# Row buffers, work between tiles, and crossed inverse rounds in a hybrid decoder trunk

## The chip, the cores and the metric

The kernel runs on one core of a Trainium2 chip. Its time is the device time of one execution in microseconds (us); lower is better. Before the change three runs gave a median of 3220.76 us (3219.93 to 3223.76).

The engines are named as the profile names them: PE is the matrix engine (PEld its weight loads), DVE the vector engine, ACT the scalar engine, POOL the general one, SP the queue that issues most transfers. Each engine runs its own instruction stream in order; the streams meet at semaphores.

## The reference, cut to what matters

One layer of a decoder with two recurrent branches. A prompt of 16 meta tokens and 512 tokens and eight samples of four tokens (560 rows in all) are normalised by rows, multiplied by one large weight matrix, sent through an RWKV-7 branch and a gated linear attention branch, merged, and projected back.

```python
h = _rms_norm(x, norm_pre[l])            # x * rsqrt(mean(x*x) + eps) * g
z = h @ w_in[l]                          # 2048 x N_COLS
...
def step(S, inp):                        # RWKV-7, one token, per head
    r_t, w_t, k_t, v_t, a_t, b_t = inp
    sa = jnp.einsum('nhvk,nhk->nhv', S, a_t)
    S = S * w_t[:, :, None, :] + sa[..., None] * b_t[:, :, None, :] + v_t[..., None] * k_t[:, :, None, :]
    return S, jnp.einsum('nhvk,nhk->nhv', S, r_t)
```

The kernel computes the RWKV recurrence by chunks of 64 tokens. Inside a chunk the terms `sa` of all tokens hang on each other through a strictly triangular 64 x 64 matrix, so each chunk needs the inverse of (identity minus that matrix), for each of 32 heads.

## The kernel before

The program is five blocks, one after the other, each closed on all engines before the next begins. Block A normalises and transposes the rows, block B projects the two low-rank columns of the RWKV branch, block C is the attention branch, block D the RWKV branch in 16 turns of two heads each, block E the output projection.

All large products are done in three passes of a split precision: a weight tile `raw` is rounded to `w_hi` by ACT (`split_hi`, L181) and the rest is put in `w_lo` by DVE (`split_lo`, L189); the activations are split likewise into `act_hi` and `act_lo`. One call of `next` on the generator `steps` (L191 to L206) issues the three matmuls of one of 16 slices of the depth, 280 columns each (L203, L204, L205). A weight tile has 32 such steps.

**Block A** (L230 to L400) goes over five tiles of 128 rows (the last has 48). There are two row buffers `x_in`. SP loads the norm's weights first, then tiles 0 and 1, and each later tile only after the tile two before it has been transposed. `square_root(t)` on ACT squares a tile in four pieces of 512 columns; DVE adds the four sums (L346); ACT takes the root (L317); DVE takes the reciprocal and scales the row (`normalise`, L349 and L353). PE transposes (L392) into four banks, ACT rounds to `act_hi` (L326), DVE subtracts to `act_lo` (L363). After the fifth tile ACT and DVE split the two first weight tiles of block B, and PE and DVE transpose and copy the small parameter vectors (L400, L373 to L379).

**Block D** is where most of the time lies. In a turn PE works through four weight tiles with `run(n)`, which issues n steps, and puts the small products of the recurrence between them, in an order that is written out by hand. Each group of small products is one call of `each` (L2050): for nine chunks and two heads one 64 x 64 product. The array is used as four quarters of 64 x 64: a product reads its operands from one half of the partitions and writes to one half of the PSUM partitions. `crossed=(a, b)` says for chunks 0 to 3 (`CROSSED`) whether head h sits in the other half on the way in (a) and out (b). With (1, 1) or for chunks 4 to 8 input and output are the same half; with (0, 1) or (1, 0) chunks 0 to 3 read one half and write the other. `CHUNK_ORDER` takes turns between the two groups of chunks.

The inverse (L2103 to L2146) begins with the diagonal 16 x 16 blocks: `n_d` and its transpose `t_d` are squared again and again (`x2`, `t2`, and back), and `inv` is multiplied by each power; ACT copies one result from PSUM, DVE copies the other and adds the product to `inv` (L1887 to L1892). Eight calls of `each` do this with `crossed=(1, 1)`. Two rounds for the whole triangle follow (L2134), which already run with (1, 0) and (0, 1). On DVE the stage starts at L1864: masks, `n_d` (L1872), `inv` (L1874, signals `inv_ready`), `t_full` minus the identity (L1876), the split of weight tile 5 (`split_lo(5)`, L1878), and the samples' sum into `af` (L1880, signals `af_ready`, for which PE waits before its second product).

Of the kernel before, what the change touches and what calls it, by code (L numbers as in the profile page):

```python
# [28 lines left out]
P = 128  # L29
D = 2048  # L30
# [27 lines left out]
DV, DS, DG = 49, 11, 5  # L58
# [32 lines left out]
def build(nc, x_prompt, x_sample, state_rwkv, state_shift, state_gla, meta_tokens, norm_pre, w_in, rwkv_mu, rwkv_w0,  # L91
# [3 lines left out]
    with ctx:  # L95
# [122 lines left out]
        x_in = [ar(D) for _ in range(2)]  # L218
        norm_row = ar(D)
# [9 lines left out]
        with nc.Block() as block:  # L229
            @block.sync  # L230
            def _(sp):
                sp.dma_start(norm_row[:, :], norm_pre[0:1, :].to_broadcast([P, D])).then_inc(load_n.sem, 16)
                for t in range(5):
                    x = x_in[t % 2]
                    if t >= 2:
                        sp.wait_ge(a_xs.sem, t - 1)
                        sp.wait_ge(a_tr.sem, 4 * (t - 1))
                    if t == 0:
                        sp.dma_start(x[0:META, :], meta_tokens[:, :]).then_inc(load_x[t].sem, 16)
                        sp.dma_start(x[META:P, :], x_prompt[0, 0:P - META, :]).then_inc(load_x[t].sem, 16)  # L240
                    elif t < 4:
# [63 lines left out]
            def _(act):  # L305
# [3 lines left out]
                def square_root(t):  # L309
                    n = rows_of[t]  # L310
                    act.wait_ge(load_x[t].sem, 16 if 0 < t < 4 else 32)
                    for g in range(4):
                        nc.scalar.activation(bank[7][0:n, :], x_in[t % 2][0:n, g * 512:(g + 1) * 512], ACT.Square,
                                             accum_out=stats[0:n, g:g + 1]).then_inc(a_ss.sem, 1)
                        act.wait_ge(a_ss.sem, a_ss.next(i))
                    act.wait_ge(a_xs.sem, 2 * t + 1)
                    nc.scalar.activation(stats[0:n, 5:6], stats[0:n, 4:5], ACT.Sqrt, scale=1.0 / D, bias=tiny[0:n, 0:1]).then_inc(a_sqrt.sem, 1)  # L317
                    act.wait_ge(a_sqrt.sem, a_sqrt.next(i))
# [10 lines left out]
                act.sem_inc(pb.half.sem, 3)  # L329
                pb.split_hi(act, 0, mine, 0, widths[0], landed=32)  # L330
                pb.split_hi(act, 0, mine, 1, widths[1], landed=48)

            @block.vector
            def _(dve):
# [8 lines left out]
                def normalise(t):  # L343
                    n, x = rows_of[t], x_in[t % 2]
                    dve.wait_ge(a_ss.sem, 4 * t + 4)
                    dve.tensor_reduce(stats[0:n, 4:5], stats[0:n, 0:4], mybir.AxisListType.X, ADD).then_inc(a_xs.sem, 1)  # L346
                    dve.wait_ge(a_xs.sem, a_xs.next(i))
                    dve.wait_ge(a_sqrt.sem, t + 1)
                    dve.reciprocal(stats[0:n, 6:7], stats[0:n, 5:6]).then_inc(mine.sem, 1)  # L349
# [2121 lines left out]
```

## Time and profile before

| | us |
|---|---|
| median of three runs | 3220.76 |
| the profiled execution | 3214.82 |
| its span | 3213.3 |
| PE busy | 3044.1 (95%) |
| DVE busy | 1700.7 (53%) |
| ACT busy | 1074.8 (33%) |
| block A, from the start to its last vector instruction | 65.1 |
| one of the 16 turns of block D, from the same line's first and last start (1084.7 and 2888.1) over 15 | 120.2 |

The profiled execution is 1.5 us longer than its span and 5.9 us (0.18%) shorter than the median. A timeline line has the start in us, the length in us, the engine, the line, the operation, and in brackets how long the engine had been idle and what released it. "issue" means that the profile shows nothing that it waited for. On PEld lines one 64 x 64 product of this type counts as two records.

### The profile page before, as it was taken

How to read it: one execution, taken by the hardware profiler on the slowest of the kernel's cores; microseconds unless marked ns; L12 is line 12 of the kernel's file. 1: busy time of each engine (PE TensorE's matmuls, PEld its weight loads, DVE VectorE, ACT ScalarE, POOL GpSimd, SP SyncE). 2: the span in 40 equal slices, each digit the busy share in tenths (PEclk: the TensorE clock that was granted, in tenths of full speed). 3: DMA queues.
4: the chain of work that ended last, by engine and by line, in shares of the span. 5: the costliest groups of instructions: out<-in, count | busy, mean ns of one | idle time of the engine just before them, and what ended most of it. 6: DMA issues, size and time to landing. Idle time of an engine off the chain costs nothing. (4 is left out here: it accounts for less than half of the span.)

```text
span 3213.3 us, 77794 instructions
## 1 busy us (share of the span) xinstructions
PE 3044.1 (95%) x33047; PEld 2802.4 (87%) x33047; DVE 1700.7 (53%) x2458; ACT 1074.8 (33%) x1832; POOL 399.4 (12%) x804
## 2 busy tenths in 40 slices
PE   4899999999998899999999999999999999996997
PEld 3898897897996899999999999999999999995897
DVE  3264454544544564664664664664664664663323
ACT  4332332432431342342342342343343343342432
POOL 2200101001002220120120120120120120111000
PEclk8999999999998999999999999999999999997998
DMA  3322423424324222222222222222222222222422
GB/s 95 99 67 84 148 66 122 122 54 145 100 53 134 62 69 58 66 69 58 66 69 58 66 69 58 66 69 58 66 69 58 66 69 61 62 68 95 132 80 99
DMA packets 368503, 255.21 MB, mean 79 GB/s; under 512 B 19380, under 2 KB 347568, under 8 KB 366256
## 3 DMA queue, kind: packets, MB, share of 16 engines
q1 hardware_dynamic: 342560, 184.18, 21.0%
q0 software_dynamic: 25600, 66.02, 6.6%
q8 instruction: 269, 4.41, 0.6%
q14 instruction: 74, 0.61, 0.1%
HBM read 212.69 MB, written 37.45 MB: 78 GB/s over the span
## 5 line engine op out<-in xcount | busy, mean ns | idle before, releaser
L203 PE MATMUL psum<-act_hi,w_hi 128*128 128x280 f32 (+2 forms) x5184 | 1587.1, 306 | 37.5 <-DVE w_lo L189 11.6
L205 PE MATMUL psum<-act_hi,w_lo 128*128 128x280 f32 (+2 forms) x5184 | 1515.8, 292 | 0.0
L204 PE MATMUL psum<-act_lo,w_hi 128*128 128x280 f32 (+2 forms) x5184 | 1514.6, 292 | 0.0
L203 PEld LDWEIGHTS psum<-act_hi,w_hi 128*128 128x128 f32 (+1 forms) x5184 | 981.3, 189 | 110.6 <-issue 69.3
L204 PEld LDWEIGHTS psum<-act_lo,w_hi 128*128 128x128 f32 (+1 forms) x5184 | 980.8, 189 | 4.5 <-issue 1.0
L205 PEld LDWEIGHTS psum<-act_hi,w_lo 128*128 128x128 f32 (+1 forms) x5184 | 980.8, 189 | 0.1
L189 DVE TENSOR_TENSOR w_lo<-raw,w_hi 128x1024 fp32r<-128x1024 f32 (+1 forms) x324 | 396.1, 1223 | 255.7 <-ACT w_hi L181 246.9
L181 ACT CAST w_hi<-raw 128x1024 fp32r<-128x1024 f32 (+1 forms) x324 | 339.4, 1048 | 41.7 <-DMA raw<-in_w_in_dram 15.1
L2056 PEld LDWEIGHTS psum<-arena 64*64 64x64 f32 x9216 | 225.6, 134 | 34.7 <-issue 34.6
L2056 PE MATMUL psum<-arena 64*64 64x64 f32 x9216 | 248.9, 221 | 7.2 <-issue 4.0
L1624 POOL DMA_DIRECT2D out_s_rwkv_dram<-arena x128 | 77.6, 614 | 1429.7 <-ACT arena L1763 1429.7
L1695 ACT ACTIVATE arena<-psum 128x280 f32<-128x280 f32 x96 | 38.9, 405 | 310.7 <-PE psum L205 309.2
L1726 ACT COPY arena<-psum 128x576 f32<-128x576 f32 x80 | 51.3, 642 | 231.5 <-PE psum L2056 231.0
L416 ACT COPY arena<-psum 128x248 f32<-128x248 f32 (+1 forms) x50 | 18.3, 367 | 262.5 <-PE psum L205 262.5
L728 ACT COPY arena<-psum 128x280 f32<-128x280 f32 x48 | 18.8, 392 | 240.0 <-PE psum L205 239.9
L1937 DVE SCALAR_TENSOR_TENSOR arena<-psum,arena 128x64 f32<-128x64 f32 x128 | 36.3, 284 | 114.9 <-PE psum L2192 114.8
L2390 DVE TENSOR_TENSOR arena<-psum,arena 128x256 f32<-128x256 f32 x32 | 13.6, 424 | 131.0 <-PE psum L2437 130.8
L1590 POOL DMA_DIRECT2D arena<-in_state_rwkv_dram x128 | 74.7, 603 | 42.8 <-DMA m_dram<-arena 37.6
L1962 DVE RECIPROCAL arena<-arena 128x560 f32<-128x560 f32 x16 | 58.5, 3654 | 38.3 <-ACT arena L1770 38.3
L779 ACT ACTIVATE arena<-psum 128x280 f32<-128x280 f32 x32 | 12.9, 404 | 195.8 <-PE psum L205 195.8
L1892 DVE TENSOR_TENSOR arena<-arena,psum 128x576 f32<-128x576 f32 x48 | 36.2, 755 | 77.1 <-PE psum L2056 76.5
L686 POOL DMA_DIRECT2D out_s_gla_dram<-arena x32 | 23.3, 727 | 418.1 <-DVE arena L1020 418.1
(328 smaller groups left out, 3362.8 us busy)
## 6 DMA issues: line engine op xcount, KB each, us to landing
raw<-in_w_in_dram SPq DMA_DIRECT2D x288, 512.0 KB, 4.4
arena<-in_state_gla_dram POOLq DMA_DIRECT2D x32, 512.0 KB, 5.3
out_s_gla_dram<-arena POOLq DMA_DIRECT2D x32, 512.0 KB, 3.3
raw<-in_w_out_dram SPq DMA_DIRECT2D x32, 512.0 KB, 4.6
ob_dram<-arena POOLq DMA_DIRECT2D x16, 280.0 KB, 3.2
arena<-ob_dram POOLq DMA_DIRECT2D x16, 280.0 KB, 4.7
m_dram<-arena POOLq DMA_DIRECT2D x16, 280.0 KB, 2.6
act_lo<-m_dram SPq DMA_DIRECT2D x1, 4200.0 KB, 14.3
```

The source lines that it names most:

```text
L181: nc.scalar.copy(w_hi[t % 2][:, ks, 0:width], raw[half][:, :, 0:width]).then_inc(self.hi.sem, 1)
L189: eng.tensor_tensor(w_lo[t % 2][:, ks, 0:width], raw[half][:, :, 0:width], w_hi[t % 2][:, ks, 0:width].bitcast(F32), SUB).then_inc(self.lo ...
L203: pe.matmul(out, hi, act_hi[:, k, cols], start=(k == 0), stop=False)
L204: pe.matmul(out, hi, act_lo[:, k, cols], start=False, stop=False)
L205: mm = pe.matmul(out, lo, act_hi[:, k, cols], start=False, stop=(k == KT - 1))
L1590: pool.dma_start(state8_in[0:C, s, :].rearrange("v (h k) -> v h k", h=2), state_rwkv[0, s, ds(2 * i, 2)].rearrange("h v k -> v h k")).then ...
L1624: pool.dma_start(s_rwkv[0, s, ds(2 * i, 2)].rearrange("h v k -> v h k"), state_out[0:C, s, :].rearrange("v (h k) -> v h k", h=2)).then_inc ...
L1695: nc.scalar.activation(tg[:, half * HALF:(half + 1) * HALF], bank[half][:, 0:HALF], ACT.Tanh, scale=0.5).then_inc(signal.sem, 1)
L1726: nc.scalar.copy(out, pair(b, 0, NC).rearrange("p (c t) -> p c t", c=NC)).then_inc(signal.sem, 1)
L1937: stt(out=states[:, c, :], in0=bank[2][:, 0:C], scalar=decays[:, c:c + 1], in1=n_t[:, c, :], op0=MUL, op1=ADD).then_inc(s_ready.sem, 1)
L1962: dve.reciprocal(e_t, e_t).then_inc(mine.sem, 1)
L2056: m = mm(out, left(c)[at], right(c)[at], start=True, stop=True)
```

## The change

It has two parts.

In block A there are five row buffers, so SP issues all loads of rows at once, tile 0 ahead of the norm's weights. ACT squares a tile in one instruction of 2048 columns, so that the reduction on DVE is gone. The parameters are prepared after tile 1 and the first weight tile is split after tile 2, and not behind the last tile. The second weight tile is split in block B.

In block D the eight inverse products run with (1, 0) or (0, 1), so that chunks 0 to 3 change halves at each. `inv` has to be in the half that the next factor is in, so `inv` for these chunks starts uncrossed (three more vector instructions), and where it is multiplied a second product with the identity carries the old `inv` over and adds it in PSUM (`keep`). DVE then copies chunks 0 to 3 and adds chunks 4 to 8, two instructions for one. The samples' sum goes ahead of `t_full` and of `split_lo(5)`, and one `run(4)` is cut in two with a product of `inv` between.

```diff
-        x_in = [ar(D) for _ in range(2)]
-        norm_row = ar(D)
+        x_in = [ar(D) for _ in range(5)]
+        norm_row, squares = ar(D), ar(D)
...
-                sp.dma_start(norm_row[:, :], norm_pre[0:1, :].to_broadcast([P, D])).then_inc(load_n.sem, 16)
                 for t in range(5):
-                    x = x_in[t % 2]
-                    if t >= 2:
-                        sp.wait_ge(a_xs.sem, t - 1)
-                        sp.wait_ge(a_tr.sem, 4 * (t - 1))
+                    x = x_in[t]
                     if t == 0:
...
+                        sp.dma_start(norm_row[:, :], norm_pre[0:1, :].to_broadcast([P, D])).then_inc(load_n.sem, 16)
...
-                    for g in range(4):
-                        nc.scalar.activation(bank[7][0:n, :], x_in[t % 2][0:n, g * 512:(g + 1) * 512], ACT.Square,
-                                             accum_out=stats[0:n, g:g + 1]).then_inc(a_ss.sem, 1)
-                        act.wait_ge(a_ss.sem, a_ss.next(i))
-                    act.wait_ge(a_xs.sem, 2 * t + 1)
...
+                    nc.scalar.activation(squares[0:n, :], x_in[t][0:n, :], ACT.Square, accum_out=stats[0:n, t:t + 1]).then_inc(a_ss.sem, 1)
...
-                pb.split_hi(act, 0, mine, 0, widths[0], landed=32)
-                pb.split_hi(act, 0, mine, 1, widths[1], landed=48)
+                    if t == 2:
+                        act.sem_inc(pb.half.sem, 3)
+                        pb.split_hi(act, 0, mine, 0, widths[0], landed=32)
...
+                    if t == 1:
+                        parameters()
+                    if t == 2:
+                        pb.split_lo(dve, 0, mine, 0, widths[0])
...
-                    tt(inv, n_d, bc(eye2, NC), ADD).then_inc(inv_ready.sem, 1)
+                    for h in range(2):
+                        tt(inv[64 * h:64 * h + 64, 0:CROSSED], gram[0:64, 0:CROSSED, h, 0:C], bc(block16[0:64], CROSSED), MUL).then_inc(mine.sem, 1)
+                        dve.wait_ge(mine.sem, mine.next(i))
+                    tt(inv[:, 0:CROSSED], inv[:, 0:CROSSED], bc(eye2, CROSSED), ADD).then_inc(mine.sem, 1)
+                    dve.wait_ge(mine.sem, mine.next(i))
+                    tt(inv[:, CROSSED:NC], n_d[:, CROSSED:NC], bc(eye2, NC - CROSSED), ADD).then_inc(inv_ready.sem, 1)
                     dve.wait_ge(inv_ready.sem, inv_ready.next(i))
-                    tt(t_full, t_full, bc(eye2, NC), SUB).then_inc(mine.sem, 1)
-                    dve.wait_ge(mine.sem, mine.next(i))
-                    pd.split_lo(dve, i, mine, 5)
                     dve.wait_ge(af_read.sem, af_read.at(i, 2))
                     tt(af[:, NF, C:P], af[:, NF, C:P], bank[5][:, 5 * C:6 * C], ADD).then_inc(af_ready.sem, 1)
                     dve.wait_ge(af_ready.sem, af_ready.next(i))
+                    tt(t_full, t_full, bc(eye2, NC), SUB).then_inc(mine.sem, 1)
+                    dve.wait_ge(mine.sem, mine.next(i))
+                    pd.split_lo(dve, i, mine, 5)
...
-                            both(lambda c, b: tt(inv[:, c, :], inv[:, c, :], b(2), ADD), inv_b)
+                            dve.tensor_copy(inv[:, 0:CROSSED], pair(2, 0, CROSSED).rearrange("p (c t) -> p c t", c=CROSSED)).then_inc(mine.sem, 1)
+                            dve.wait_ge(mine.sem, mine.next(i))
+                            tt(inv[:, CROSSED:NC], inv[:, CROSSED:NC], pair(2, CROSSED, NC - CROSSED).rearrange("p (c t) -> p c t", c=NC - CROSSED),
+                               ADD).then_inc(inv_b.sem, 1)
...
-                            for h in range(2):
-                                out = pair(b, c, 1)[half_of(c, h, crossed[1])]
-                                at = half_of(c, h, crossed[0])
-                                m = mm(out, left(c)[at], right(c)[at], start=True, stop=True)
+                            for identity in ((False, True) if keep and c < CROSSED else (False,)):
+                                for h in range(2):
+                                    out = pair(b, c, 1)[half_of(c, h, crossed[1])]
+                                    at = half_of(c, h, crossed[0])
+                                    m = mm(out, eye2[at] if identity else left(c)[at], right(c)[at], start=not identity,
+                                           stop=identity or not keep or c >= CROSSED)
...
-                    each(6, of(t_d), of(n_d))
+                    each(6, of(t_d), of(n_d), crossed=(1, 0))
...
-                    each(4, of(n_d), of(t_d), inv_mm)
+                    each(4, of(n_d), of(t_d), inv_mm, crossed=(1, 0))
...
-                    each(6, of(t2), of(x2))
-                    each(4, of(x2), of(t2))
-                    each(2, of(t2), of(inv), inv_mm)
-                    run(4)
+                    each(6, of(t2), of(x2), crossed=(0, 1))
+                    each(4, of(x2), of(t2), crossed=(0, 1))
+                    run(2)
+                    each(2, of(t2), of(inv), inv_mm, crossed=(0, 1), keep=True)
+                    run(2)
...
-                    each(6, of(n_d), of(t_d))
-                    each(2, of(t_d), of(inv), inv_mm)
+                    each(6, of(n_d), of(t_d), crossed=(1, 0))
+                    each(2, of(t_d), of(inv), inv_mm, crossed=(1, 0), keep=True)
...
-                    each(2, of(x2), of(inv), inv_mm)
+                    each(2, of(x2), of(inv), inv_mm, crossed=(0, 1), keep=True)
```

## Rows read from the trace of the kernel before

**Rows 1.** The page, part 1: busy us (share of span) and instructions.

```profile
PE 3044.1 (95%) x33047; PEld 2802.4 (87%) x33047; DVE 1700.7 (53%) x2458; ACT 1074.8 (33%) x1832; POOL 399.4 (12%) x804
```

**Rows 2.** Timeline of SP's queue in block A.

```profile
1.05 0.40 SPq L232 DMA_DIRECT2D arena<-in_norm_pre_dram  x1
...
2.43 25.74 SPq L242 DMA_DIRECT2D arena<-in_x_prompt_dram  x3
```

**Rows 3.** Transfers issued in the first 12 us: KB each, us to landing.

```profile
arena<-in_norm_pre_dram SPq DMA_DIRECT2D x1, 1024.0 KB, 5.5
arena<-in_x_prompt_dram SPq DMA_DIRECT2D x1, 1024.0 KB, 11.1
```

**Rows 4.** Timeline of ACT, DVE and PEld in block A and the first of B.

```profile
10.73 1.28 ACT L313 ACT_TABLE_LOAD   x1 [10.73 <-DMA arena<-in_x_prompt_dram]
...
12.03 0.60 ACT L313 ACTIVATE psum<-arena 128x512 f32<-128x512 f32 x1
...
15.35 1.28 ACT L317 ACT_TABLE_LOAD   x1 [0.34 <-DVE arena L346]
...
16.64 0.29 ACT L317 ACTIVATE arena<-arena,tiny 128x1 f32<-128x1 f32 x1
...
17.24 2.35 DVE L353 SCALAR_TENSOR_TENSOR arena<-arena 128x2048 f32<-128x2048 f32 x1
...
41.16 2.87 DVE L363 TENSOR_TENSOR act_lo<-psum,act_hi 128x512 fp32r<-128x512 f32 x4
...
49.45 4.45 DVE L363 TENSOR_TENSOR act_lo<-psum,act_hi 128x512 fp32r<-128x512 f32 x8
...
54.64 2.22 DVE L189 TENSOR_TENSOR w_lo<-raw,w_hi 128x896 fp32r<-128x896 f32 x2 [0.75 <-ACT w_hi L181]
...
62.89 0.55 DVE L373 COPY params<-psum 128x128 f32<-128x128 f32 x2
...
64.89 0.17 DVE L379 TENSOR_SCALAR derived<-params 128x16 f32<-128x16 f32 x1
...
65.88 0.26 PEld L203 LDWEIGHTS psum<-act_hi,w_hi 128*112 128x112 f32 x1 [2.20 <-issue]
```

**Rows 5.** Busy time by stretch; after POOL's the granted clock (1.00 is 2.4 GHz).

```profile
66.00:69.30 3.30, 3.30 (x15) 3.30 (x16) 0.00 (x0) 0.00 (x0) 0.28 (x2) 0.50 0.03 5
```

**Rows 6.** Timeline of PE's weight loads in the inverse of turn 6.

```profile
1809.10 1.13 PEld L2056 LDWEIGHTS psum<-arena 64*64 64x64 f32 x36 [0.17 <-issue]
...
1814.03 3.23 PEld L2056 LDWEIGHTS psum<-arena 64*64 64x64 f32 x108 [0.15 <-issue]
...
1819.18 2.21 PEld L2056 LDWEIGHTS psum<-arena 64*64 64x64 f32 x72 [0.27 <-issue]
...
1823.20 1.13 PEld L2056 LDWEIGHTS psum<-arena 64*64 64x64 f32 x36 [0.15 <-issue]
1825.75 1.24 PEld L2056 LDWEIGHTS psum<-arena 64*64 64x64 f32 x72 [0.16 <-issue]
1829.02 0.69 PEld L2056 LDWEIGHTS psum<-arena 64*64 64x64 f32 x36 [0.37 <-issue]
```

**Rows 7.** Timeline of DVE in the same stretch.

```profile
1805.05 1.92 DVE L1872 TENSOR_TENSOR arena<-arena 64x256 f32<-64x256 f32 x4
1807.00 0.76 DVE L1874 TENSOR_TENSOR arena<-arena 128x576 f32<-128x576 f32 x1
...
1808.59 2.49 DVE L189 TENSOR_TENSOR w_lo<-raw,w_hi 128x1024 fp32r<-128x1024 f32 x2
1811.11 0.22 DVE L1880 TENSOR_TENSOR arena<-arena,psum 128x64 f32<-128x64 f32 x1
...
1817.52 0.76 DVE L1890 COPY arena<-psum 128x576 f32<-128x576 f32 x1 [3.92 <-PE psum L2056]
1818.31 0.76 DVE L1892 TENSOR_TENSOR arena<-arena,psum 128x576 f32<-128x576 f32 x1
```

**Rows 8.** Timeline of ACT in the same stretch.

```profile
1809.29 1.51 ACT L1722 COPY arena<-psum 128x512 f32<-128x512 f32 x3 [2.88 <-PE psum L2101]
```

More of the change, by code:

```diff
@@ L57 @@
 ZW = 1 + TP + NSEQ * (TS + 1)
-DV, DS, DG = 49, 11, 5
+DV, DS, DG = 55, 11, 5
 DED = 2
@@ L352, in normalise, with parameters @@
                         dve.wait_ge(load_n.sem, 16)
-                    dve.scalar_tensor_tensor(out=x[0:n, :], in0=x[0:n, :], scalar=stats[0:n, 6:7], in1=norm_row[0:n, :],
+                    dve.scalar_tensor_tensor(out=x[0:n, :], in0=x[0:n, :], scalar=stats[0:n, 10 + t:11 + t], in1=norm_row[0:n, :],
                                              op0=MUL, op1=MUL).then_inc(a_xs.sem, 1)
                     dve.wait_ge(a_xs.sem, a_xs.next(i))
+                def parameters():
+                    for n in range(5):
+                        dve.wait_ge(a_par.sem, n + 1)
+                        w = [P, 64, P, P, P][n]
+                        out = params[:, n * P:n * P + w] if n < 2 else shift_in[:, (n - 2) * P:(n - 1) * P]
+                        dve.tensor_copy(out, bank[4 + n % 3][:, 0:w]).then_inc(a_parc.sem, 1)
+                        dve.wait_ge(a_parc.sem, a_parc.next(i))
+                    dve.tensor_copy(shift_in[0:LORA, 384:400], params[0:LORA, 176:192]).then_inc(mine.sem, 1)
+                    dve.wait_ge(mine.sem, mine.next(i))
+                    dve.tensor_scalar(derived[:, 0:32], params[:, W0:W0 + 32], 0.5, None, MUL).then_inc(mine.sem, 1)
+                    dve.wait_ge(mine.sem, mine.next(i))
+                    dve.tensor_scalar(derived[:, 32:48], params[:, K_A:K_A + 16], -1.0, 1.0, MUL, ADD).then_inc(mine.sem, 1)
+                    dve.wait_ge(mine.sem, mine.next(i))
                 normalise(0)
@@ L461, in _ @@
                 mine, i = s_order, 0
+                pb.split_hi(act, 0, mine, 1, widths[1], landed=48)
                 for half in range(2):
@@ L474, in _ @@
                 mine, i = v_order, 0
+                pb.split_lo(dve, 0, mine, 1, widths[1])
                 for t in range(2):
@@ L1878, in turn_of @@
                     pd.split_lo(dve, i, mine, 5)
-                    dve.wait_ge(af_read.sem, af_read.at(i, 2))
-                    tt(af[:, NF, C:P], af[:, NF, C:P], bank[5][:, 5 * C:6 * C], ADD).then_inc(af_ready.sem, 1)
-                    dve.wait_ge(af_ready.sem, af_ready.next(i))
                     def both(op, signal):
@@ L2048, in half_of, with each @@
                         return head[1 - h if crossed and c < CROSSED else h]
-                    def each(b, left, right, signal=None, crossed=(1, 1)):
+                    def each(b, left, right, signal=None, crossed=(1, 1), keep=False):
                         for c in CHUNK_ORDER:
-                            for h in range(2):
-                                out = pair(b, c, 1)[half_of(c, h, crossed[1])]
-                                at = half_of(c, h, crossed[0])
-                                m = mm(out, left(c)[at], right(c)[at], start=True, stop=True)
+                            for identity in ((False, True) if keep and c < CROSSED else (False,)):
[4 more added lines that the diff above has]
+                                           stop=identity or not keep or c >= CROSSED)
                         if signal:
```

47 lines of the change are left out of this document (19 added, 28 removed).

## Prediction

> **What bounds the kernel now.** I read the page's busy times first: PE is busy for 95% of the span and no other engine for more than 53% [rows 1]. Over most of the kernel, then, only two things count: what PE executes, and what it waits for. Next I read where PE is not busy. The largest stretch that this change touches is block A: PE's first large product starts at 65.88, and what ends the block is DVE's last parameter instruction, at 64.89 + 0.17 = 65.06 [rows 4]. Everything behind is closed off by a block end, so what block A gives up goes off the span one for one. Then I read one turn of block D on PE's weight loads. Between products of different tile shapes there is always a gap of 0.15 to 0.17; only what goes beyond that is a wait. In turn 6 the inverse has three such gaps: 0.33 ahead of its second product (its start, 1811.44, is the sum's end, 1811.11 + 0.22, plus 0.11), 0.27 and 0.37 [rows 6, 7]. So in the inverse PE is nearly always at work, and shorter products are time saved as long as DVE and ACT keep up.
>
> **Block A, the start.** Now the norm's megabyte goes first and lands at 1.05 + 5.5 = 6.6 [rows 2, 3]; tile 0 lands at 10.73, where ACT begins [rows 4]. With tile 0 first the same megabyte should be there at about 7.0. Tile 1 has as many bytes ahead of it as before and lands at 2.43 + 11.1 = 13.5 [rows 2, 3]. ACT then needs the table (1.28), the square, the second table (1.28) and the root (0.29) [rows 4]. A square of 2048 columns isn't in the trace; 512 take 0.60 [rows 4], so it lies between 0.6 and 2.4, and I take 2.1, with 0.1 for its sum, because nearly all of the 0.60 is columns. The root is there at 12.2, and DVE's scaling (0.2 + 2.35 [rows 4]) ends at 14.8, where it ended at 19.6.
>
> **Block A, the rest.** Tile 1 is squared from 13.5 on and its root is there at 16.1. From there the engine that is late is DVE: a tile costs it 2.55 to scale and 2.87 to subtract [rows 4], 5.4 in all; ACT needs 2.2 + 0.3 + about 2.4 = 4.9 and no longer waits for loads. Its list is four scalings (10.2), the subtractions of tiles 0 to 2 (8.6), the parameters (from 62.89 to 65.06, 2.17 [rows 4]), the first weight split (2.22 [rows 4]) and the last two tiles' subtractions (4.45 with their waits on PE and ACT [rows 4]): 27.6, so the end lies at 43.8, and with some handovers at 44 to 45. Against 65.06 that is 20 to 21. I take **20**. If tile 0 landed no sooner than now, 3.7 of it would go; if sooner still, 1.5 come on top: 16.5 to 21.5. The parameters' wait on PE holds PE's next transposes behind it, but DVE reaches the parameters only at about 27, ten after POOL's last issue. The first weights now queue behind all five tiles on SP; they are wanted at about 32 and cost nothing while that holds. The split of the second tile, two times about 2 on ACT and DVE, moves into block B, where PE works 13 on the first tile: hidden, and worth at most 2 if not. Block B begins with the clock at 0.50 for 3.4 [rows 5]; if the denser transposes kept it up, 1.7 more would be saved. I take nothing, as PE still has pauses of some 4 ahead of it.
>
> **Block D, the price of a product group.** An uncrossed group is 36 records in 1.13; a crossed pair is 72 in 1.24, one alone 0.69 [rows 6]. The reason shows in the counts: uncrossed, nine products go through each of two quarters, 1.13 / 9 = 0.126 each; crossed, five at most through each of four, 0.63. Five groups are simply crossed: 0.45 to 0.5 each. Three carry identity products, 52 records; the trace has none of that kind. The off-diagonal quarters then take eight products each, 8 x 0.126 = 1.01. The ends are 0.95 (52 records at 0.69 / 36 [rows 6]) and 1.63 (52 at 1.13 / 36 [rows 6]); I take 1.05, nearest to the crossed row, which has the same quarters. So the identity eats nearly all of the gain there.
>
> **Block D, followed through turn 6.** DVE has `n_d` at 1805.05 + 1.92 = 1806.97 [rows 7]. Two 64 x 256 instructions (0.48 each [rows 7]) and two of about 256 and 320 columns (0.45 and 0.52, between these and the 0.76 of 576 columns [rows 7]) put `inv_ready` at 1808.95. PE wants it at 1809.10 [rows 6]: the three added instructions are just hidden; beyond that each costs its length. The sum is now ready at 1809.2, so the second product waits for ACT's copies, 1809.29 + 1.51 = 1810.80 [rows 8], and starts at 1810.91 rather than 1811.44. It ends at 1811.60. DVE, though, has `t_full` and the split (0.79 + 2.49 [rows 7]) in front of the copy of `t2`: free at 1812.5, copy done at 1813.3, PE goes on at 1813.4, 0.4 after its own steps end. Against 1814.03 [rows 6] the turn is 0.6 ahead.
>
> The pair takes 1.24, two steps and the gap 1.0, the product with `inv` 1.05: it ends at 1816.7. A copy starts 0.26 after such an end (1814.03 + 3.23 to 1817.52 [rows 6, 7]). DVE then needs 0.79 for `t_d`, 0.45 and 0.52 for the two parts of `inv`: done at 1818.75, and PE, which has only two steps left to hide this instead of four, is ready at 1817.75 and waits 1.1. It starts at 1818.85 against 1819.18 [rows 6]: only 0.33 ahead. **This wait, and the one of 0.4, take the place of the 0.17 and 0.11 that there are now.** The next pair takes 0.62 + 1.05 where it took 2.21, four steps hide DVE (1.26 of work under 1.8), the last product saves 0.08, and the whole-triangle rounds start at 1824.81 against 1825.75 [rows 6]: 0.94. The gap of 0.37 ahead of 1829.02 [rows 6] comes from ACT's split of tile 6, which PE's own 32nd step releases; it moves along, and 0.94 stays. Behind it PE has steps to issue all the way to the turn's end, so nothing gives it back. Sixteen turns: **15**. Splitting tile 5 later (its end moves by 1.4) holds SP's next load by as much, but those weights are wanted 12 later.
>
> **The sum.** 20 + 15 = 35 off the profiled execution, 3214.8 (span 3213.3), gives 3180. The median of the runs stands 5.9 higher, and I take 35 off that: **3186**. The bounds: block A 16.5 to 21.5, with the clock 23; a turn 0.94 with each identity group at 1.05. At 0.95 each, 1.2 a turn; at 1.63, 0.94 - 3 x 0.58 = -0.8.
>
> **Rivals.** *Identity at the uncrossed pitch*: -0.8 a turn, +13, with block A -20: 3214. The crossed row speaks against it.
>
> *Off-diagonal products can't overlap*, the rival on the slower side. Where the two row halves write the same bank, the products might go one by one, sixteen of them at 0.126: 2.0 for each of the three identity groups. That adds 3 x 0.98 - 0.94 = 2.0 a turn, 32, less 20: 3233. The change turns slower from about 1.8 per identity group. The crossed row of 0.69 speaks against it, since there too two row halves write one bank; it holds only if accumulating over the identity is different. The Trainium skill, TensorEngine Tiling, Restrictions and Gotchas, says for row tiling that different row tiles cannot access the same PSUM bank at the same time. By that rule even an uncrossed group would take 18 x 0.126 = 2.3; the trace has 1.13 [rows 6], so the trace does not agree for tiles that write different partitions.
>
> *The crossing is eaten whole*: if DVE's two added instructions or `inv_ready` come 0.5 later than I put them in each turn, PE waits for them at three places with under 0.15 to spare, and the 0.94 is gone: 3201. For it speaks that spare; against it that the two `inv` instructions are no longer than worked out from rows.
>
> *The waits don't come*: if DVE's copy of `t_d` and `inv` were hidden after all, a turn saves 0.94 + 1.1 + 0.4 = 2.4, 39 in all: 3162. Nothing hides it that I can see.
>
> *The change doesn't start sooner*: tile 0 lands as late as now: 3190, inside the range.
>
> **How the numbers follow.** My forecast with its bounds (3177 to 3196) gets 0.73, the crossing eaten whole 0.11, the waits that don't come 0.07, the identity at the uncrossed pitch 0.05, products one by one 0.04. The range goes from 3176 to 3202. A measurement of this kernel can tell about 0.2% (6.4) from no change, so faster means below 3214.3: 0.93 (the forecast, the two on its sides and some of the uncrossed pitch); within: 0.03; slower: 0.04.
>
> **What would show it.** Right: PE's first L203 at 44.5 to 48 rather than 65.88; ACT's first table load at about 7; turns of 119.3 rather than 120.2; crossed groups of 0.69 and identity groups of about 1.05 on PEld; a gap of over 1.0 ahead of the round that multiplies `t_d` by `inv`, and one of about 0.5 ahead of the round before it. Wrong: a first table load at 10.7, identity groups over 1.3, a gap at the first product of the inverse, or no long gap after the two steps.

## The result and the profile after

The changed kernel took a median of 3184.3 us over four runs (3177.2 to 3190.7) against 3220.4 for the kernel before: ratio 0.989, 95% interval 0.987 to 0.991, 36 us less. The forecast was 3186, 35 less. The profiled execution took 3177.2 with a span of 3175.7, where the one before had 3214.8 and 3213.3; the two spans differ by 37.6. It is the fastest of the four, so the medians give the whole and the trace the parts.

The page of the changed kernel, part 1: busy us, share of the span, instructions.

```profile
PE 3004.8 (95%) x33815; PEld 2760.3 (87%) x33815; DVE 1723.9 (54%) x2549; ACT 1070.5 (34%) x1802; POOL 397.8 (13%) x804
```

Against [rows 1] PE has 768 more records and is busy 39 us less. The records are the identity products: 24 a turn, two records each, sixteen turns. They add work, and yet the sum of PE's work falls, because eighteen crossed products take 0.66 to 0.69 where eighteen uncrossed ones took 1.13 [rows 6].

The timeline of block A in the changed kernel; the rows answer to [rows 4].

```profile
7.43 1.28 ACT L309 ACT_TABLE_LOAD   x1 [7.43 <-DMA arena<-in_x_prompt_dram]
8.72 1.91 ACT L309 ACTIVATE arena<-arena 128x2048 f32<-128x2048 f32 x1
...
12.04 0.29 ACT L311 ACTIVATE arena<-arena,tiny 128x1 f32<-128x1 f32 x1
12.91 1.91 ACT L309 ACTIVATE arena<-arena 128x2048 f32<-128x2048 f32 x1 [0.58 <-DMA arena<-in_x_prompt_dram]
...
27.41 0.55 DVE L353 COPY params<-psum 128x128 f32<-128x128 f32 x2
...
35.10 2.22 DVE L189 TENSOR_TENSOR w_lo<-raw,w_hi 128x896 fp32r<-128x896 f32 x2
...
39.92 4.45 DVE L368 TENSOR_TENSOR act_lo<-psum,act_hi 128x512 fp32r<-128x512 f32 x8
...
45.19 0.26 PEld L203 LDWEIGHTS psum<-act_hi,w_hi 128*112 128x112 f32 x1 [1.85 <-issue]
```

Tile 0 is there at 7.43 and not at 10.73; DVE's last subtraction ends at 44.4; PE's first large product starts at 45.2 and not at 65.9. That is 20.7 us.

Turn 6 of block D in the changed kernel, PE's weight loads; the rows answer to [rows 6].

```profile
1783.72 0.66 PEld L2064 LDWEIGHTS psum<-arena 64*64 64x64 f32 x36 [0.17 <-issue]
1785.68 0.69 PEld L2064 LDWEIGHTS psum<-arena 64*64 64x64 f32 x36 [0.42 <-issue]
1787.96 1.27 PEld L2064 LDWEIGHTS psum<-arena 64*64 64x64 f32 x72 [0.32 <-issue]
1790.27 1.02 PEld L2064 LDWEIGHTS psum<-arena 64*64 64x64 f32 x52 [0.16 <-issue]
1793.44 1.57 PEld L2064 LDWEIGHTS psum<-arena 64*64 64x64 f32 x88 [1.26 <-issue]
1796.82 1.02 PEld L2064 LDWEIGHTS psum<-arena 64*64 64x64 f32 x52 [0.15 <-issue]
1799.27 1.24 PEld L2064 LDWEIGHTS psum<-arena 64*64 64x64 f32 x72 [0.15 <-issue]
```

The groups of 36 records take 0.66 to 0.69 where they took 1.13; the ones with identity products (52 records) take 1.02. The gap of 1.26 is new: 1.1 us of waiting beyond the 0.15 to 0.17 that each change of tile shape costs.

DVE in the same stretch; the rows answer to [rows 7].

```profile
1781.61 0.87 DVE L1873 TENSOR_TENSOR arena<-arena 64x256 f32<-64x256 f32 x2
1782.52 0.42 DVE L1875 TENSOR_TENSOR arena<-arena 128x256 f32<-128x256 f32 x1
1782.98 0.49 DVE L1877 TENSOR_TENSOR arena<-arena 128x320 f32<-128x320 f32 x1
1783.51 0.22 DVE L1880 TENSOR_TENSOR arena<-arena,psum 128x64 f32<-128x64 f32 x1
1783.77 0.76 DVE L1882 TENSOR_TENSOR arena<-arena 128x576 f32<-128x576 f32 x1
1784.56 2.49 DVE L189 TENSOR_TENSOR w_lo<-raw,w_hi 128x1024 fp32r<-128x1024 f32 x2
1787.08 0.76 DVE L1893 COPY arena<-psum 128x576 f32<-128x576 f32 x1
1791.58 0.76 DVE L1893 COPY arena<-psum 128x576 f32<-128x576 f32 x1 [3.75 <-PE psum L2064]
1792.38 0.42 DVE L1895 COPY arena<-psum 128x256 f32<-128x256 f32 x1
1792.84 0.49 DVE L1897 TENSOR_TENSOR arena<-arena,psum 128x320 f32<-128x320 f32 x1
```

`inv` is begun in three more instructions and ends at 1783.47, and PE's first product starts at 1783.72 with the usual gap: hidden, as said. The last three rows are the new wait: they end at 1793.33, and PE goes on at 1793.44.

Over all turns, the first mask line (`t_d`) gives the mean length: its first and last start, over 15. The line's answer in the kernel before, then in the changed one:

```profile
L1868 DVE TENSOR_TENSOR arena<-arena x16: 759/759/761, 1082.0 to 2885.4; 128x576 f32<-128x576 f32 x16
```

```profile
L1866 DVE TENSOR_TENSOR arena<-arena x16: 759/759/761, 1062.7 to 2850.1; 128x576 f32<-128x576 f32 x16
```

That is 120.23 and 119.16, 1.07 less a turn. From turn to turn the distance varies: 119.90 to 120.92 before, 118.80 to 120.62 after. The shortest turns differ by 1.10; what lies above the shortest is pauses on PE of another kind, told at the end. Below, both numbers stand, since the shortest turn shows the schedule and the mean what an execution paid.

The span, cut at PE's first product of block B, at the first product of block D and at the first of block E (65.9, 1036.7 and 2961.8 before; 45.2, 1017.5 and 2926.3 after): block A -20.7, blocks B and C +1.5, block D -16.3, block E -2.1, together -37.6. The change doesn't touch block E, and its 2.1 is no larger than the scatter: in the twelve profiles block E takes 249.2 to 252.4.

### The profile page after: what moved, and what is told of

Read it like the earlier page. It is cut to its first block and busy times, and to the rows that moved or that the text cites. A ratio compares the mean times of both kernels' runs of the same rounds, so it can differ in the third digit from the quotient of the medians.

```text
span 3175.7 us, 79378 instructions
## 1 busy us (share of the span) xinstructions
PE 3004.8 (95%) x33815; PEld 2760.3 (87%) x33815; DVE 1723.9 (54%) x2549; ACT 1070.5 (34%) x1802; POOL 397.8 (13%) x804
## 5 line engine op out<-in xcount | busy, mean ns | idle before, releaser
L203 PE MATMUL psum<-act_hi,w_hi 128*128 128x280 f32 (+2 forms) x5184 | 1588.9, 307 | 39.9 <-issue 12.9
L2064 PE MATMUL psum<-arena 64*64 64x64 f32 x9984 | 209.2, 223 | 24.0 <-DVE arena L1897 13.8
L2064 PEld LDWEIGHTS psum<-arena 64*64 64x64 f32 x9984 | 183.9, 134 | 54.8 <-issue 54.7
L777 ACT ACTIVATE arena<-psum 128x280 f32<-128x280 f32 x32 | 12.9, 404 | 195.4 <-PE psum L205 195.4
L1018 DVE SCALAR_TENSOR_TENSOR arena<-arena,psum 128x512 f32<-128x512 f32 x64 | 47.8, 747 | 52.4 <-PE psum L1315 50.4
```

Of the source, the lines that this page charges most:

```text
L203: pe.matmul(out, hi, act_hi[:, k, cols], start=(k == 0), stop=False)
L1018: stt(out=sstate[s % 3][:, n, :], in0=sstate[s % 3][:, n, :], scalar=ends[:, n, GN + s:GN + s + 1], in1=bank[4 + n], op0=MUL, op1=ADD).the ...
L2064: m = mm(out, eye2[at] if identity else left(c)[at], right(c)[at], start=not identity, stop=identity or not keep or c >= CROSSED)
```

## Experiments: the two parts by themselves

**Block A alone.** The diff's edits up to the split of the first weights; the inverse is that of before.

> Only the edits in block A; the inverse is that of before. Theory (the two parts add up): PE's first large product starts at 45 to 46 instead of 65.9 and nothing behind gives it back: 20 us less, ratio 0.9936 to 0.9942, a turn still 120.2. Rival (the gain is given back where block C loads its first weights, or the whole gain comes from the turns): first product at 45 as well, but the ratio at 0.998 or above.

Measured: 3194.0 us, ratio 0.9919 (0.9896 to 0.9941). PE's first product starts at 45.03; turns are 120.13 on average and 119.90 at the shortest, those of before. The two parts are separate, and nothing gives back what block A saves. The ratio reads as 26 us, more than was expected, the trace as 20.9; the interval (19 to 33 us) covers both.

**Block D alone.** The diff's edits from L1872 of the changed kernel on; block A is that of before.

> Only the edits in block D; block A is that of before. Theory: a turn takes 119.1 to 119.3 instead of 120.2 and the sixteen make 15 to 17 us, ratio 0.9945 to 0.9955. Rival (the crossing is eaten whole by waits for the vector engine, and what the changed kernel gained beyond block A is scatter between runs): a turn of 120.0 or more, ratio above 0.998.

Measured: 3205.3 us, ratio 0.9960 (0.9949 to 0.9971). The line of `t_d` in this kernel:

```profile
L1868 DVE TENSOR_TENSOR arena<-arena x16: 758/759/761, 1089.5 to 2878.0; 128x576 f32<-128x576 f32 x16
```

A turn of 119.23, 118.81 at the shortest. So the crossing is not eaten whole. The ratio is 13 us, a little under the 15 to 17 expected; the trace's turns give 16. The span of this execution is only 6.1 shorter than that of before, mostly because its blocks B and C took 978.1, 7.2 more than before: the granted clock was 0.50 for 53 us of them, where it was so for 39.

## Experiments: what in block A saves the time

**Buffers alone.** The changed kernel with the work between tiles behind the last tile again.

```diff
-                    if t == 1:
-                        parameters()
-                    if t == 2:
-                        pb.split_lo(dve, 0, mine, 0, widths[0])
+                for t in range(2):
+                    pb.split_lo(dve, 0, mine, t, widths[t])
+                parameters()
```

On ACT both `split_hi` and on PE the parameters' transposes go behind the loop in the same way.

> The changed kernel with the parameters and both first weight splits behind the last tile again; the five buffers, the one square and the order of loads are kept. Theory (block A is as long as the list of what the vector engine still has to do): the last subtraction ends at 40, both splits with the second tile's load and the parameters take as long behind it as before (11), and PE's first large product starts at 51 to 53 instead of 45.2: of the 20.7 about 14 come from loads and squares, 7 from moving work between the tiles. Rival (the loads are all of it): first product at 46 or before.

Measured, PE's weight loads and DVE in block A of that kernel:

```profile
52.09 0.26 PEld L203 LDWEIGHTS psum<-act_hi,w_hi 128*112 128x112 f32 x1 [2.20 <-issue]
```

```profile
39.66 0.36 DVE L368 TENSOR_TENSOR act_lo<-psum,act_hi 128x192 fp32r<-128x192 f32 x1 [0.36 <-ACT act_hi L320]
40.77 2.22 DVE L189 TENSOR_TENSOR w_lo<-raw,w_hi 128x896 fp32r<-128x896 f32 x2 [0.75 <-ACT w_hi L181]
46.08 0.96 DVE L189 TENSOR_TENSOR w_lo<-raw,w_hi 128x768 fp32r<-128x768 f32 x1 [3.10 <-ACT w_hi L181]
```

The last subtraction ends at 40.0, and behind it come 11 us, with 3.1 of waiting for the second tile's load. Of the 20.7, 13.8 come from loads, buffers and the square, 6.9 from moving work between the tiles. ACT in the kernel before:

```profile
28.41 0.60 ACT L313 ACTIVATE psum<-arena 128x512 f32<-128x512 f32 x1 [4.34 <-DMA arena<-in_x_prompt_dram]
...
43.15 0.59 ACT L313 ACTIVATE psum<-arena 48x512 f32<-48x512 f32 x1 [2.21 <-DMA arena<-in_x_sample_dram]
```

There it waits 6.6 for tiles 2 and 4, which were asked for only when a buffer was free; these waits are gone.

**Norm first.** The changed kernel with the norm's load ahead of tile 0.

```diff
+                sp.dma_start(norm_row[:, :], norm_pre[0:1, :].to_broadcast([P, D])).then_inc(load_n.sem, 16)
                 for t in range(5):
                     x = x_in[t]
...
-                        sp.dma_start(norm_row[:, :], norm_pre[0:1, :].to_broadcast([P, D])).then_inc(load_n.sem, 16)
```

> The changed kernel with the norm's weights loaded ahead of tile 0 again. Theory: tile 0 lands at 10.7, its root is there at 15.4, tile 1 (landed long before) at 17.9 instead of 14.95, and every later step of block A moves by the same 2.5 to 3: PE's first large product at 47.7 to 48.3 instead of 45.2. Rival (the start is hidden by later waits, since tile 1 lands at 13 either way): 45.2 to 45.7.

Measured, ACT in block A and PE's first product:

```profile
11.20 1.28 ACT L309 ACT_TABLE_LOAD   x1 [11.20 <-DMA arena<-in_x_prompt_dram]
```

```profile
48.97 0.26 PEld L203 LDWEIGHTS psum<-act_hi,w_hi 128*112 128x112 f32 x1 [1.85 <-issue]
```

Tile 0 lands 3.8 later and block A ends 3.8 later: one megabyte ahead of the first tile passes through to the end in full. I had expected 2.5 to 3, with tile 0 at 10.7 and not at 11.2. So of the 13.8, 3.8 are the order of two loads. The other 10.0 belong to the five buffers and the one square together; no run parts these two.

## Experiments: what in block D saves it, and what it costs

**The sum ahead, by itself.** The kernel before with one move.

```diff
+                    dve.wait_ge(af_read.sem, af_read.at(i, 2))
+                    tt(af[:, NF, C:P], af[:, NF, C:P], bank[5][:, 5 * C:6 * C], ADD).then_inc(af_ready.sem, 1)
+                    dve.wait_ge(af_ready.sem, af_ready.next(i))
                     tt(t_full, t_full, bc(eye2, NC), SUB).then_inc(mine.sem, 1)
                     dve.wait_ge(mine.sem, mine.next(i))
                     pd.split_lo(dve, i, mine, 5)
-                    dve.wait_ge(af_read.sem, af_read.at(i, 2))
-                    tt(af[:, NF, C:P], af[:, NF, C:P], bank[5][:, 5 * C:6 * C], ADD).then_inc(af_ready.sem, 1)
-                    dve.wait_ge(af_ready.sem, af_ready.next(i))
```

> The kernel before with nothing but the samples' sum put ahead of t_full and the split. Theory: PE's second product loses the 0.17 that it waited over the change of tile shape, a turn of 120.0 to 120.1, 2 to 4 us, ratio 0.9988 to 0.9994. Rival (the split moves into the way of the copy of t2): the gap ahead of the first pair of squarings opens and the time stays or grows, ratio 1.000 or more.

Measured: ratio 0.9982 (0.9973 to 0.9992), turns of 119.82, 119.68 at the shortest. By the shortest turn the move is worth 0.22, near the 0.17 expected; the mean fell by 0.40, because this execution also had fewer pauses. The ratio, 6 us, lies beyond the 2 to 4 expected, and its interval reaches back to them.

**The sum behind the split, in the changed kernel.** The reverse move.

> The changed kernel with the samples' sum behind t_full and the split of weight tile 5 again, everything else kept. Theory: the sum is ready at 2.49 + 0.79 later, PE's second product waits for it about 1.7 longer, but the split is then out of the way of the copy of t2, which gives 0.2 back: a turn of 120.3 to 120.7, 18 to 25 us above the changed kernel, ratio to before 0.995 to 0.997. Rival (the order of the two makes no difference, since the vector engine has to do both before the copy of t2): the same time as the changed kernel, ratio 0.989.

Measured: 3219.2 us, ratio 1.0006 (0.9993 to 1.0018). PE's weight loads in turn 6:

```profile
1799.53 0.69 PEld L2064 LDWEIGHTS psum<-arena 64*64 64x64 f32 x36 [1.90 <-issue]
...
1801.64 1.24 PEld L2064 LDWEIGHTS psum<-arena 64*64 64x64 f32 x72 [0.16 <-issue]
...
1803.93 0.19 PEld L2064 LDWEIGHTS psum<-arena 64*64 64x64 f32 x2 [0.16 <-issue]
1804.78 1.02 PEld L2064 LDWEIGHTS psum<-arena 64*64 64x64 f32 x50 [0.66 <-issue]
```

Ahead of the second product the gap is 1.90, and the wait ahead of the first pair is gone (0.16). The schedule did what was expected: the shortest turns, 120.11, are 1.3 above 118.80. But the mean turn is 121.37, 2.2 above, and this is no accident of one execution: the ratio over ten runs lies 0.0114 above the changed kernel's, 37 us or 2.3 a turn, where 18 to 25 us were expected. What lies above the shortest turns is in about equal parts pauses, such as the 0.66 inside a group, and the clock. PE in turn 3, 1.6 behind the end of its gap of 1.90, and the busy time of a stretch there with the granted clock behind POOL's column:

```profile
1437.96 2.21 PEld L2064 LDWEIGHTS psum<-arena 64*64 64x64 f32 x72 [0.27 <-issue]
```

```profile
1437.00:1440.40 3.40, 3.40 (x78) 3.02 (x77) 0.13 (x1) 0.00 (x0) 0.00 (x0) 0.50 0.58 160
```

The granted clock falls to 0.50 for 3.4 us, and the pair of squarings takes 2.21 where turn 6 has 1.24. This happens in turns 0, 3, 5, 7, 9, 14 and 15; turns 3, 5 and 7, which have no long pause, take 121.6, 1.5 above the shortest. In the changed kernel's profile the clock stays at 1.00 from 1040 to 2900, all but the end of the last turn. The mean granted clock of these ten runs is 0.971 to 0.976, that of the changed kernel's four 0.977 to 0.980.

What it tells of the change: **without the move of the sum, the crossing makes the turn no shorter at all.** The three added instructions that begin `inv` would stand in front of the sum with `t_full` and the split, and PE would wait for it. In the schedule the move is worth 0.2 by itself and 1.3 under the crossing; in the runs it is worth 2.3 there, because the long gap also costs clock.

**Without the identity.** The changed kernel without the second product of the three `keep` groups; the old inverse isn't carried over for chunks 0 to 3, so this part of the computation is left out.

```diff
-                            for identity in ((False, True) if keep and c < CROSSED else (False,)):
+                            for identity in (False,):
...
-                                           stop=identity or not keep or c >= CROSSED)
+                                           stop=True)
```

> The changed kernel without the identity products (the old inverse is not carried over for chunks 0 to 3, so that part of the computation is left out). Theory (eight products in a row through each off-diagonal quarter set the length of the three groups): these groups fall from 1.02 to 0.66 to 0.72, and since PE has steps to issue, the turn loses nearly three times that, 0.8 to 1.1: the shortest turns go from 118.80 to 117.7 to 118.0. Rival (the vector engine's copy and add behind each group are what PE waits for, and the groups' length is hidden): the shortest turns stay at 118.6 or more.

Measured, the first such group in turn 6:

```profile
1785.59 0.66 PEld L2064 LDWEIGHTS psum<-arena 64*64 64x64 f32 x36 [0.15 <-issue]
```

The shortest turn falls from 118.80 to 117.74, by 1.06: three times 0.36, within rounding. In the schedule the identity products are paid in full, 17 us over the sixteen turns, about as much as the whole part in block D saves; the mean turn of this one execution fell by 0.82.

**Four steps behind.** The one product that was put between two times two steps goes back ahead of four.

```diff
-                    run(2)
                     each(2, of(t2), of(inv), inv_mm, crossed=(0, 1), keep=True)
-                    run(2)
+                    run(4)
```

> The changed kernel with the two steps ahead of the product of t2 and inv put behind it again, so that four steps hide the vector engine's three instructions. Theory (the wait of 1.26 ahead of the round that multiplies t_d by inv is there because two steps are shorter than those three instructions): the gap falls to 0.4 to 0.6, a turn takes 118.0 to 118.2 instead of 119.2, 16 us below the changed kernel, ratio to before 0.983 to 0.985. Rival (the vector engine is late for another reason, its split or its copies, and the wait moves along): gap of 1.2 again and the same time as the changed kernel, ratio 0.989.

Measured: 3177.3 us, ratio 0.9865 (0.9839 to 0.9892). PE's weight loads in turn 6:

```profile
1792.20 2.39 PEld L2064 LDWEIGHTS psum<-arena 64*64 64x64 f32 x124 [0.32 <-issue]
...
1796.74 1.57 PEld L2064 LDWEIGHTS psum<-arena 64*64 64x64 f32 x88 [0.49 <-issue]
```

The gap falls from 1.26 to 0.49, and the shortest turns are 117.61, 1.19 under the changed kernel's. So the wait was there because two steps are shorter than DVE's three instructions. The mean turn, 118.61, is only 0.55 lower, though, and the ratio shows no clear step from 0.989: the expectation of 16 us missed. Most of the rest can be read turn by turn. In turns 3, 8 and 13 both kernels have a pause of the kind told at the end, just ahead of the wait. Turn 3 in the changed kernel, then here:

```profile
1435.01 0.19 PEld L203 LDWEIGHTS psum<-act_hi,w_hi 128*128 128x128 f32 x1 [1.67 <-issue]
```

```profile
1439.67 0.19 PEld L203 LDWEIGHTS psum<-act_hi,w_hi 128*128 128x128 f32 x1 [2.81 <-issue]
```

In the changed kernel the three pauses (1.67, 1.32, 1.25) take the place of the wait: the gap of 1.26 is 0.15 in these turns, which lie only 0.47, 0.23 and 0.42 above its shortest. Here the pauses (2.81, 1.99, 1.94) have hardly a wait to hide in, and in turn 3 the granted clock falls to 0.50 for 3.4 us behind the pause; the three turns lie 4.00, 1.86 and 1.88 above the shortest. The difference, 6.6, is most of the 9.5 us that fifteen turns lack. The wait that was filled had been covering other stops.

**Waits filled.** Four steps behind, and three more moves.

```diff
-                    pe.wait_ge(inv_b.sem, inv_b.at(i, 3))
+                    pe.wait_ge(inv_b.sem, inv_b.at(i, 2))
                     pe.sem_inc(waited.sem, 1)
                     each(6, of(n_d), of(t_d), crossed=(1, 0))
+                    pe.wait_ge(inv_b.sem, inv_b.at(i, 3))
+                    pe.sem_inc(waited.sem, 1)
...
-                    pd.split_lo(dve, i, mine, 5)
+                    pd.split_lo(dve, i, mine, 5, halves=(0,))
...
+                        if n == 0:
+                            pd.split_lo(dve, i, mine, 5, halves=(1,))
...
                     each(6, of(t_d), of(n_d), crossed=(1, 0))
-                    run(2)
+                    run(3)
...
                     each(4, of(n_d), of(t_d), inv_mm, crossed=(1, 0))
-                    run(3)
+                    run(2)
```

> Four steps behind as in the run before, and three more edits: the round's first product waits only for the copy of t_d and not for inv; one half of the split of weight tile 5 stands behind the copy of t2; one step goes from behind the second product to ahead of it, where PE waits for the copies of b_k. Theory (PE takes every wait in the inverse as time of its own): the gaps ahead of the second product, of the second pair and of the round of t_d go to 0.15 to 0.25, a turn takes 117.4 to 117.7, 25 to 28 us below the changed kernel, ratio to before 0.979 to 0.982. Rival (what is filled here comes up as a wait in the rounds of the whole triangle, behind the scalar engine's split of tile 6): no faster than the run with four steps alone.

Measured: 3156.2 us, ratio 0.9809 (0.9785 to 0.9834), the fastest kernel of this study, 28 below the changed one (27 by the ratios), as expected. PE's weight loads in turn 6, and the line of `t_d`:

```profile
1780.43 0.66 PEld L2066 LDWEIGHTS psum<-arena 64*64 64x64 f32 x36 [0.16 <-issue]
...
1782.24 2.15 PEld L2066 LDWEIGHTS psum<-arena 64*64 64x64 f32 x124 [0.27 <-issue]
...
1786.21 1.54 PEld L2066 LDWEIGHTS psum<-arena 64*64 64x64 f32 x88 [0.16 <-issue]
```

```profile
L1866 DVE TENSOR_TENSOR arena<-arena x16: 758/759/761, 1069.3 to 2830.4; 128x576 f32<-128x576 f32 x16
```

The three gaps are 0.16, 0.27 and 0.16 (the second just above the 0.15 to 0.25 expected), the mean turn 117.41, the shortest 116.92: 1.9 under the changed kernel. Of that, 1.2 are the four steps and 0.7 the three moves; against the run before, the gaps shrink by 0.26, 0.05 and 0.33. Nothing came up instead in the rounds of the whole triangle, whose gaps are 0.16, 0.36, 0.15 and 0.16 here and 0.15, 0.35, 0.15 and 0.15 in the changed kernel.

## Why the prediction was right

**Block A, 20 expected, 20.7 measured.** Its steps held one by one. Tile 0 was there at 7.4 (7.0 said), the first root at 12.3 (12.2), tile 1 squared from 12.9 (13.5), and from then on DVE was the last to be ready, but for one wait of 1.1 on ACT: its list ended at 44.4 (43.8 plus handovers). The square of 2048 columns, put between 0.6 and 2.4, took 1.91, 2.01 with the reading of its sum, where I took 2.1. The rival in which the start is not sooner is out (7.43), and `norm_first` shows what it would have cost, 3.8 (3.7 said).

The clock in block B, put at no change with a gain of 1.7 as the other end, went the other way. Busy time by stretch of the changed kernel, the granted clock behind POOL's column:

```profile
45.00:48.40 3.40, 3.18 (x14) 3.21 (x15) 1.92 (x2) 1.61 (x2) 0.49 (x3) 0.50 0.02 5
48.40:52.00 3.60, 3.60 (x25) 3.60 (x25) 0.00 (x0) 0.00 (x0) 0.00 (x0) 0.80 0.00 0
```

It stays at 0.50 to about 49.8 (a mean of 0.80 over 3.6 is 1.4 at 0.5), 4.7 after the first product. In the kernel before it rose 3.7 after it, at 69.5, a little later than the 3.4 of the prediction. That costs 0.5, a bound that I hadn't set. It is part of the 1.5 that blocks B and C take longer; the rest is no larger than the scatter of these blocks between executions (970 to 981 from B's first to D's first product in twelve profiles, among kernels that differ there only in where the second weight tile is split). The four profiles at 978 to 981 are those with the granted clock at 0.50 for 53 to 58 us of these blocks; the others have 38 to 45.

**Block D, 15 expected, 16.3 measured.** A turn was worked out at 0.94 and is 1.07 on average, 1.10 at the shortest. Term by term: crossed groups 0.66 to 0.69 (0.62 to 0.69 said), identity groups 1.02 (1.05), so the reckoning by products in a row through a quarter, 8 x 0.126, held for a kind of group that the trace of before didn't have. The Trainium skill, TensorEngine Tiling, Restrictions and Gotchas, with its rule that row tiles can't share a PSUM bank at one time, would have made these groups twice as long; 1.02 for sixteen products that go to one bank from both row halves does not agree with it. This rests on 0.126 as the price of one product in one quarter. At half that price the groups would fit the rule too, one row half at a time. Another group of eighteen products in the changed kernel decides it, which reads one row half alone (partitions 64 to 127) and writes both:

```profile
1779.01 1.13 PEld L2102 LDWEIGHTS psum<-arena 64*64 64x64 f32 x36 [0.16 <-issue]
```

Nine go through each of its two quarters, and 1.13 / 9 is 0.126 again. No two row halves compete there; at half the price it would have taken 0.57. The two rivals on longer identity groups are out by the 1.02.

The new wait ahead of the round of `t_d` was said to be 1.1 and is 1.11 (1.26 less 0.15). The wait of 0.4 ahead of the pair of squarings was mis-sized: it is 0.17 (0.32 less 0.15). DVE's four short instructions took 1.86 with their gaps where 1.93 was put, and PE's second product started 1.96 behind the first where 1.81 was worked out, with a gap of 0.42 for ACT's copies; so DVE's copy was less late and PE got there later. From the first product to the first round of the whole triangle PE took 15.55 (1783.72 to 1799.27) where 15.71 was worked out; of the 0.16 gained, about half came up to the pair of squarings and the rest from the identity groups, 0.03 each.

**What was not seen.** The move of the sum is in the prediction's path (the sum ready at 1809.2, the second product waiting for ACT's copies instead), but without a price of its own. By itself it is worth 0.22 a turn; that it also carries the crossing, at 1.3 in the schedule and 2.3 in the runs, wasn't said. The step "the three added instructions are just hidden" held for the first product with either order (a gap of 0.17 in both). For the second product it holds only with the sum ahead of the split.

**Luck.** The pauses and the falls of the clock in block D have no term in the prediction. In the two profiles compared they nearly cancel: what lies above the shortest turn is 0.32 before and 0.36 after. In the runs with the sum behind the split and with four steps behind it is 1.27 and 0.99, and there expectations made in the same way missed.

## What to carry to other kernels

Where PE has work for every moment, read the schedule of its small products as two lists: how many of them go in a row through each quarter of the array, and how long the engine that feeds the next group takes against the steps that stand between. A change that shortens the first list shortens the cover of the second as well, and then the order on the feeding engine (here one small sum in front of a long split) decides whether anything is left. In a preparing block, count what the slowest engine still has to do after the first data lands; here a megabyte ahead of the first tile passed through in full, 3.8 us at both ends. And don't price a wait by its length alone: one that is filled may have covered another, and behind a long stop of PE the clock fell in some turns.

## What the runs showed of the hardware that was not expected

**Pauses on PE.** In single turns PE stops for 0.5 to 2.8 us at an instruction for which the profile names no releaser, inside a group of small products or in the steps right behind one. Many were at the same instruction of the same turn in kernels with the same block D. PE's weight loads in the changed kernel and in block D alone:

```profile
2150.70 1.57 PEld L2064 LDWEIGHTS psum<-arena 64*64 64x64 f32 x88 [1.26 <-issue]
...
2166.43 0.31 PEld L2064 LDWEIGHTS psum<-arena 64*64 64x64 f32 x12 [0.66 <-issue]
```

```profile
2192.79 0.31 PEld L2066 LDWEIGHTS psum<-arena 64*64 64x64 f32 x12 [0.60 <-issue]
```

Both have 24 of a group's 36 records before them and 12 behind; `buffers_alone` has 0.53 and `norm_first` 1.07 at the same record.

What PE waits for is in the traces' lists of transfers. The page of the changed kernel has a queue with its packets, megabytes and share of the transfer engines' time:

```profile
q8 instruction: 275, 4.51, 0.6%
```

These are packets of 16 KB. The kernel before has 269; the six more go with 768 more weight loads and as many matmuls, 256 instructions a packet, and the changed kernel without the identity products has 269 again. So this queue brings PE's instructions. In the first fifteen turns of the twelve traces there are 68 pauses of over 0.45 that most turns do not have at the same record. All 68 end 1.25 to 1.55 us after one of these packets has landed, while the packets come 9.5 us apart on average. So **PE stands still because its next instructions have not arrived.** Ahead of the 21 pauses of over 1 us, the weight transfers kept the transfer engines busy for 72% or more of the 2 us before the packet began; some of the shorter pauses have no such traffic ahead of them.

**Half the weight bytes** in block D were tried against this:

```diff
-                        load_rwkv(sp, i, t)
+                        col = TILES[t % 6] + t // 6 * P
+                        for half in range(2):
+                            sp.wait_ge(pd.lo.sem, pd.lo.at(i, 2 * t - 1 + half))
+                            sp.sem_inc(waited.sem, 1)
+                            sp.dma_start(raw[half][:, 0:KT // 4, :], w_in[0, half * D // 2:half * D // 2 + D // 4, ds(i * P + col, P)].rearrange(
+                                "(k p) c -> p k c", p=P)).then_inc(pd.loaded[half].sem, 16)
```

> The changed kernel, block D loading only half of each weight tile's rows (the other half keeps what an earlier tile left, so the products aren't those of the reference). Turns of the changed kernel take 118.80 to 120.62, and what lies above the shortest is pauses of 0.6 to 1.2 on PE inside a group of small products, for which the profile shows no releaser, at times when the weight transfers keep all transfer engines busy. Theory (the pauses come from those transfers, which something that PE needs has to queue behind): with half the bytes they go, the mean of the turns is 118.8 to 118.95 and none is over 119.2. Rival (they have nothing to do with the weight transfers): mean of 119.1 or more, with single turns over 119.5.

Measured: a mean turn of 119.03, the longest 119.50, so neither number of the theory was met (118.95 and 119.2), and the mean misses the rival's too. But the pauses are shorter. In turn 3 the four kernels with this block D stop for 1.67 to 1.94 at one record, and this one for 0.84; in turn 8 they stop for 1.32 to 1.85, and this one for 0.22. At the record shown above there is no gap, and inside the groups none is over 0.27. It is one execution, but the same at each of these records: the weight transfers make these pauses longer. With the busy share ahead of the packets this fits packets that are held up behind the weights. Why some packets come late without such traffic stays open.

What lies above the shortest turn is 0.3 us a turn in the kernel before, 0.4 in the changed one, 1.0 in `four_steps_behind` (with one fall of the clock) and 0.5 in `waits_filled`, and was not forecast.

**The granted clock inside block D.** It fell to 0.50 (1.2 GHz) nine times in the twelve traces: seven times in `sum_behind_split` and once each in `norm_first` and `four_steps_behind`. Each fall came 1.0 to 1.7 us after the end of a stop of PE of 1.9 to 2.8 us and lasted 3.4 us. Behind other stops of about 1.9 us, such as that of turn 6 above, it stayed at 1.00; what decides between them is not shown.
